# One in-projection pass for blocks 4 to 7, and a work timetable levelled for TensorE, in a hybrid attention and expert-retrieval kernel

## The reference

```python
h = rmsnorm(x)                                   # per token
q, k, v, xc, B, C = split(h @ w_in, 6)           # w_in: 1024 x 3072
sb = stick_breaking(rmsnorm(q), rmsnorm(k), v)   # 8 heads of 64, strictly causal
cv = B * causal_depthwise_conv3(C * xc)          # 512 channels
x = x + concat(rmsnorm(sb), rmsnorm(cv)) @ w_out
h2 = rmsnorm(x)
s1, s2 = (h2 @ w_q) against two tables of 128 sub-keys, for 8 heads
idx, gate = top 16 of the sums of the top 16 + 16, softmax over them
x = x + sum over 8 x 16 picks: gate * gelu(peer_u[idx] . h2) * peer_v[idx]
```

## Time and profile before

| | |
|---|---|
| median of 3 runs | 2874.86 us |
| the profiled execution: its time, and its span | 2879.8 us, 2878.0 us |
| busy: PE, DVE, ACT, POOL | 77%, 69%, 38%, 38% of the span |
| bytes moved by DMA | 1183.89 MB, mean 411 GB/s |
| of these by the gathers (q0), by SP's queue (q1) | 1073.81 MB, 108.17 MB |
| first dot | 104 us after the span's start |
| granted clock of TensorE, mean | 0.893 |

### The profile page before, as it was taken

How to read it: one execution, slowest core, us unless ns; L and a number is a source line. 1 busy time by engine, 2 the same in 40 slices (tenths; PEclk the granted TensorE clock), 3 DMA queues, 4 the chain that set the end, 5 groups by cost and what they waited for, 6 DMA issues and landing times. The chain is left out here.

```text
span 2878.0 us, 29917 instructions
## 1 busy us (share of the span) xinstructions
PE 2225.2 (77%) x9210; PEld 1012.2 (35%) x9210; DVE 1983.9 (69%) x4782; ACT 1093.7 (38%) x3164; POOL 1103.9 (38%) x1037
## 2 busy tenths in 40 slices
PE   9788889778977887778986888777898656555555
PEld 6535525333532343333542244333354111111111
DVE  3757766787666668786767666888666666666654
ACT  2333432552333335562333334666233322322222
POOL 0333433343343334443344333444334444434442
PEclk9999999989998998899998999999999776777787
DMA  9999999999999999999999999999999999999998
GB/s 390 359 413 403 398 419 418 419 412 412 385 421 420 419 419 412 419 415 416 412 420 420 418 410 416 410 417 415 419 405 420 416 422 419 421 418 416 415 421 353
DMA packets 178865, 1183.89 MB, mean 411 GB/s; under 512 B 19856, under 2 KB 21520, under 8 KB 47632
## 3 DMA queue, kind: packets, MB, share of 16 engines
q0 software_dynamic: 147456, 1073.81, 90.5%
q1 hardware_dynamic: 31248, 108.17, 9.6%
HBM read 1177.70 MB, written 4.19 MB: 411 GB/s over the span
## 5 line engine op out<-in xcount | busy, mean ns | idle before, releaser
L1472 DVE CUSTOM_DVE_ANT_0 ring<-ring,h2r 128x1024 f32<-128x1024 f32 x1024 | 1249.0, 1223 | 781.2 <-DMA ring<-table_uv,idx_t 772.1
L643 POOL DMA_INDIRECT ring<-table_uv,idx_t x1024 | 1102.0, 1076 | 1755.0 <-DVE dots L1472 1128.9
L911 PE MATMUL acc<-ring,wmask 128*64 128x512 f32 x4096 | 1200.6, 715 | 578.2 <-ACT wmask L1069 574.2
L911 PEld LDWEIGHTS acc<-ring,wmask 128*64 128x64 f32 x4096 | 283.4, 153 | 1286.4 <-ACT wmask L1069 845.9
L1064 ACT ACTIVATE dots<-dots 128x2 f32<-128x2 f32 x512 | 104.1, 203 | 1530.5 <-DVE dots L1472 1528.0
L1069 ACT ACTIVATE wmask<-gmask,dots 128x64 f32<-128x64 f32 x1024 | 300.3, 340 | 48.6 <-ACT dots L1064 1.5
L1057 ACT ACTIVATE gmask<-stack,gate_t 128x64 f32<-128x64 f32 x1024 | 293.1, 334 | 0.6 <-DVE gate_t L1459 0.5
L666 PE MATMUL pt<-hT,w_held 128*128 128x256 f32 (+1 forms) x560 | 109.3, 344 | 0.0
L666 PEld LDWEIGHTS pt<-hT,w_held 128*128 128x128 f32 x560 | 88.2, 193 | 28.2 <-issue 21.1
L1064 ACT ACT_TABLE_LOAD x73 | 93.7, 1283 | 1.3
L657 PE MATMUL pz<-w_ring,hT 128*128 128x512 f32 x192 | 90.8, 615 | 0.0
(11 more groups left out here) (274 smaller groups left out, 2171.6 us busy)
## 6 DMA issues: line engine op xcount, KB each, us to landing
w_ring<-wstream SPq DMA_DIRECT2D x121, 512.0 KB
ring<-wstream SPq DMA_DIRECT2D x32, 512.0 KB, 11.7
ring<-table_uv,idx_t POOLq DMA_INDIRECT x1024
w_held<-wstream SPq DMA_DIRECT2D x11, 512.0 KB, 13.4
xs<-x_in_dram SPq DMA_DIRECT2D x8, 512.0 KB
h2r<-wstream SPq DMA_DIRECT2D x8, 512.0 KB, 14.8
scores<-wstream SPq DMA_DIRECT2D x8, 512.0 KB, 15.4
xs<-wstream SPq DMA_DIRECT2D x4, 512.0 KB, 12.3
```

What stands on the lines that cost most here:

```text
L643: nc.gpsimd.indirect_dma_start(out=ring[:, cell(t):cell(t) + 2, :].rearrange("p c d -> p (c d)"), out_offset=None, in_=table, in_offset=ba ...
L911: mm = nc.tensor.matmul(acc[HALF * i:HALF * i + HALF, half * 512:(half + 1) * 512], wmask[:, slot, :], ring[:, cell(2 * p + i) + 1, half * ...
L1472: V.tensor_tensor_reduce(u, u, h2r[:, b % H_SLOTS, i, :], 1.0, 0.0, ALU.mult, ALU.add, dots[:, t % SLOTS:t % SLOTS + 1]).then_inc(dots_don ...
```

## The change

The in-projection (pieces 0 to 23) of supers 3 and 4 is made in one pass, in super 3 (`WIDE`), over its four blocks; super 4 (`LAST`) begins with its attention. In the pass each piece is used in four parts instead of two. The convolution works on 512 tokens at a time, and its steps stand before those of v (`ORDER`).

Room for the two additional blocks: their turned h lies in the parts of `kT` and `vals_sb` that belong to blocks 6 and 7 (`ahead_turned`), so the two pieces that were parked there for super 3 (33 and 36) are streamed. `cvT` and `qT` grow to four blocks, and `w_held` shrinks from 11 to 9 pieces (`LENT = 2`): pieces 37 and 38 lie in the new halves of `cvT` and `qT` up to super 2, and are streamed in supers 3 and 4. x of blocks 6 and 7 is loaded there for the pass (the step `ahead`), and a second time where it was loaded before, for the residual.

The stream has 103 pieces: 24 fewer for super 4, two more each for supers 3 and 4, and two more for super 3. With the two additional loads of x there are 16 transfers of 512 KB fewer.

`WHEN` gives super 2 less time (up to 212 and 254 instead of 224 and 262), super 3 begins at tick 254 instead of 262, super 4 at 524 instead of 521. `levelled()` is new: it takes the spread steps and moves a step to a later tick when TensorE's work, at 2.68 us a tick of which 0.97 us are the mix, would run more than 2.85 us behind.

```diff
-WHEN = [(-1, -1, 16), (8, 66, 84), (72, 224, 262), (262, 470, 514), (521, 732, 775)]
+WHEN = [(-1, -1, 16), (8, 66, 84), (72, 212, 254), (254, 473, 514), (524, 726, 775)]
+PART = 4.6
-H2_AT = {3: 266, 5: 518, 7: 790}
+H2_AT = {3: 260, 5: 518, 7: 790}
+ORDER = [list(range(PIECES)) for _ in SUPER]
+ORDER[WIDE] = [*range(PIECE_V), *range(PIECE_CONV, PIECE_OUT), *range(PIECE_V, PIECE_CONV), *range(PIECE_OUT, PIECES)]
+ORDER[LAST] = list(range(PIECE_OUT, PIECES))
+def parts_of(f, j):
+    return 4 if f == WIDE and j < PIECE_OUT else SUPER[f]
 def home(f, j):
-    if j >= FIRST_HELD:
+    if j >= FIRST_HELD + LENT or j >= FIRST_HELD and f < WIDE:
         return "held", j - FIRST_HELD
...
-        if f <= room + 1:
+        if f <= min(room + 1, WIDE - 1):
...
 def front_steps(f):
+    main = [(0.0, ("ahead",))] if f == WIDE else []
+    main += [(1.0, ("norm", blocks[0]))] if f != LAST else []
+    for b in blocks[1:] if f != LAST else ():
+        main += [pause(X_LATE if b >= X_SLOTS + 2 else 0), (1.0, ("norm", b))]
+    if f == WIDE:
+        main += [(1.0, ("norm", b)) for b in AHEAD]
+        main += [pause(1), (6.0, ("root1", blocks[0])), pause(4)]
+        for pair in (blocks, AHEAD):
+            main += [(2.0, ("h_scale", b)) for b in pair]
+        for pair in (blocks, AHEAD):
+            main += [pause(1)] + [(3.0, ("h", b)) for b in pair] + [(3.0, ("hT", b)) for b in pair]
+        main += [pause(1)] + w(*range(PIECE_K)) + [pause(1)] + w(*range(PIECE_K, PIECE_V)) + [pause(1)]
...
+        for c in range(1, CH):
+            j = PIECE_CONV + 3 * c
+            main += w(j, j + 1, j + 2) + [(4.0, ("conv", c))]
+        main += w(*range(PIECE_V, PIECE_CONV)) + [pause(1)] + [(3.0, ("qk_turn", b)) for b in AHEAD]
...
+TENSOR_TIME = {"w": 1.85, "v": 1.85, "scores": 1.8, "values": 1.4, "turn": 1.6, "h": 1.0, "qk_turn": 0.9, "x_turn": 1.1,
+               "key_scores": 1.4, "part": 0.3}
+TENSOR_TICK, TENSOR_SUM, TENSOR_LATE = 2.68, 0.97, 1.0
+def levelled(wanted):
+    out, queues, late = {}, [[] for _ in SUPER], 0.0
+    for tick in sorted(wanted):
+        for step in wanted[tick]:
+            queues[step[0]].append((tick, step))
+    for tick in range(min(wanted), BLOCKS * PICKS):
+        late = max(0.0, late + TENSOR_SUM - TENSOR_TICK) if tick >= 0 else 0.0
+        for queue in queues:
+            while queue and queue[0][0] <= tick:
+                step = queue[0][1]
+                needs = TENSOR_TIME.get(step[1], 0.0) if tick >= 0 else 0.0
+                if needs and late + needs > TENSOR_LATE + TENSOR_TIME["w"]:
+                    break
+                if step[1] == "h" and step[0] and queues[step[0] - 1]:
+                    break
+                late += needs
+                out.setdefault(tick, []).append(step)
+                queue.pop(0)
+    return out
...
 # ScalarE
-                if name == "norm":
+                if name == "norm" and i > 1:
+                    act.wait_ge(ahead_in, 32)
+                    act.wait_ge(piece_done, done(f - 1, PIECES - 1))
+                    nc.scalar.activation(spare[i - 2], lent[i - 2], ACT.Square, accum_out=ss1[:, i:i + 1]).then_inc(x_squared, 1)
+                elif name == "norm":
...
 # VectorE
                 if name == "root1":
-                    dve.wait_ge(x_squared, b0 + n)
-                    inverse_root(inv1[:, 0:n], ss1[:, 0:n], n, 1.0 / D, done=norm1)
+                    dve.wait_ge(x_squared, made_to(f))
+                    inverse_root(inv1[:, 0:made(f)], ss1[:, 0:made(f)], made(f), 1.0 / D, done=norm1)
 # SyncE
+                if name == "ahead":
+                    sp.wait_ge(piece_done, done(f - 1, FIRST_HELD + LENT - 1))
+                    for i, b in enumerate(AHEAD):
+                        sp.dma_start(lent[i], x[b * P:(b + 1) * P, :]).then_inc(ahead_in, 16)
```

277 lines of the change are left out of this document (177 added, 100 removed).

## The result

Five runs each: 2889.59 us (2889.3 to 2894.44) against 2874.86 (2872.92 to 2875.57), a ratio of 1.0051 [1.004, 1.0063]. The forecast was 2856, the range 2842 to 2869. The profiled execution took 2894.4 us (span 2892.6), 14.6 above that of before.

The account below looks back on a forecast made before the run. Gathers at 421 GB/s were taken as the bound. Terms -19.9 - 3.5 - 4.0 + 2 + 7 + 4 - 5 = -19.4 us from the profiled 2879.8, less 4.9, gave 2856 us; range 2842 to 2869.

Parts of the forecast that it names:

- Bytes: Whole kernel: 16 transfers fewer, 8.39 MB at 421 GB/s, shorten the time by 19.9 us.
- End of super 1: From tick 48: levelling spreads TensorE's pieces over 42 ticks, gain 3.5 us; bounds 6.5 gain to 3 loss.
- signs of being wrong: Below 400 GB/s in super 3's attention, no dip at tick 258, or super 1's end as slow as before.
- Attention of super 2: Eight passes in 31 ticks instead of 48, DVE's same passes in less room: adds 2 us, bounds 0 and 6.
- End of super 2: Key scores six ticks earlier, so DVE's wait for them goes: gain 4.0 us, bounds 5.2 and 0.
- Start of super 3: Tick 258: ACT waits for block 5's x before its norm, and the DMA queues run dry: 7 us lost, bounds 0 and 12.
- Super 3: In-projection stays DMA-bound, attention loses 0.3 us a pass, 8 with the handover against 4.2 before: loss 4 us.
- Super 4: 48 parts fewer and attention in 143 ticks instead of 98: gain 5 us, bounds 8 and 0.
- super 3 gives it back: Rival: super 3's attention pass costs 0.8 us more than the gathers, 13 us, its start 12: 2869 us; chance 0.11.
- an attention in series: Rival: super 3's passes can't overlap, 13.7 us each, 99 us in the place of 5: 2950 us; chance 0.03.
- first view: DMA row with GB/s below: DMA share stands at 9 in every slice while GB/s runs from 359 to 422.

Follow-up runs that it names:

- run 13: The changed kernel with the last 16 streamed pieces of weights loaded twice each, one load after the other: 2913.3 us, ratio 1.0143.
- run 2: The changed kernel without the levelling of TensorE's steps, all else as changed: 2876.20 us, ratio 1.0003.
- run 15: The kernel of run 14 without the rooms of two or three ticks written in by hand: 2869.16 us, ratio 0.9984.
- run 14: The changed kernel with block 5's norm four ticks later, levelling budget 2.85 us, super 3's parts closer, and rooms of two or three ticks: 2865.71 us.
- run 1: The changed kernel with the norm of block 5 five ticks later, tick 263 in the place of 258: 2879.39 us, ratio 1.0011.
- run 3: The changed kernel with block 4's first stick at least five ticks behind its scores, and the convolution's sums four pieces earlier: 2884.37 us, ratio 1.0025.
- run 5: The changed kernel with a levelling that never puts a step without TensorE work nearer to the step ahead than the timetable wanted: 2898.74 us, ratio 1.0074.
- run 10: The changed kernel with levelling budget 2.85 us and super 3's handover four ticks later, its distances kept: 2885.22 us, ratio 1.0049.
- run 11: The changed kernel with levelling budget 2.85 us, both second-pair q and k transposes in tick 382, scores, stick and sums one tick later: 2879.94 us, ratio 1.0027.
- run 12: The changed kernel with super 3's second scores three ticks behind the first, tick 389 for 387, first stick and sums following: 2880.71 us, ratio 1.0025.
- run 9: The changed kernel with only the first scores of super 3 four ticks later, tick 390 in the place of 386: 2877.96 us, ratio 1.0016.

## Why the prediction was wrong

*Bytes, -19.9.* Right: 20.0 by the bytes of the table, 16 to 26 by run 13, which adds a little lateness to the bytes. A stage that loses nothing moves 421 GB/s here too (the window from 720.8). The Trainium skill, "DMA: Bandwidth & Descriptors", section Bandwidth, gives about 358 GB/s, by which the bytes would be an estimated 23.4 us; but the same section gives that figure for two cores that stream at once, and measured 425 on one core alone. This kernel runs on one core, so the trace disagrees with the reading in the prediction and not with the section.

*End of super 1, -3.5.* Wrong: +1.8 in the first profile, +0.3 by the mean of seven, and 391 GB/s as before, which was one of the prediction's own signs of being wrong. I had priced it as load over time, 0.17 us a tick too much for TensorE (by its own terms 93.7 us in 35 ticks, 2.68 a tick and not 2.66). Levelling spreads the load over more ticks and doesn't change the loss: 6.7 us without it (run 2), 6.9 with it. So the load of a tick doesn't set it; what does stays open.

*Attention of super 2, +2 (bounds 0 to 6).* Mis-sized: 7 to 9. Run 2 gives back 3 of it, the room of two ticks before the last sum of squares 4 (ticks 176 to 192 lose 5.6 us in run 15 and 1.5 in run 14, which adds the rooms). There `sb_turn` and `sb_sum` stand in one tick, TensorE waits 3.5 us for ACT's square and mixes at 3.68 us behind it. I had priced DVE's busy time and no wait.

*End of super 2, -4.* Right in mechanism, -5.8: the scores wait is gone, and nothing took its place. In run 2 the key scores stand early too, without the levelling, and 3.4 us are lost there: by these losses the earlier scores are worth 2.7 and the levelling 3.1.

*Start of super 3, +7 (0 to 12).* Right in mechanism, mis-sized: 11.8, and run 1 removes it. I let the queues refill with the dot of tick 259, after 5.2 us without bytes. They were empty or nearly so for some 7 us, and thin for 12 us more, in which POOL waits once again (3.3 us lost, which I had at under 2). The landing time was 8.4 us (issue 851.47, ACT 859.89), as in the earlier trace rows. The Trainium skill, same page, section "Anatomy of one DMA", has 2.0 us and the bytes at 436 GB/s for a transfer that GpSimd issues; x is loaded by SP. Taken as an estimate here it would be 3.2 us, and this term nothing; the trace has 8.4 beside full queues, and that decides.

*Super 3, +4 (-2 to +15).* The step that failed: the overlap at the handover from in-projection to attention, of which the sum had at most 3 us. Of my 8 us, 16 passes of 0.3 made 5 and the handover with the in-projection 3. It was the other way round: ticks 400 to 432, at three ticks a pass, lose 0.3 us in all, so the pace that I feared is free in this kernel; handover and in-projection lose 23.3, the handover alone 17.2, and all of super 3 is +21.5, outside the bound. The in-projection's part is the first convolution step (4.9 us), where DVE's wider steps, which the prediction put at nothing, hold up ACT and by it the mix. I had compared each engine's busy time with the gathers' pace, and not read the order of tick 385 to 387: ACT, transpose, ACT, transpose, scores, mix, then ACT again, scores, sums, and the next mix only behind them. Runs 3 and 5 excluded the stick's distance as the only cause, run 10 the place, run 11 the shared tick, and run 12 the backlog as the only cause; what is left, was forecast for run 12 (3 to 7 us; 7.3 measured, with a time nearly 3 us over the 2878 expected) and shows in POOL's rows is two mixless stretches in a row. Why the loss is 10 in one kernel and 17 in another isn't settled by their lengths alone (run 3 has 14.6 and 14.8 us and loses 10.1, run 5 has less and loses 12.3), and the clock's part isn't separated.

*Super 4, -5.* -5.1 from tick 544 on, all of it ahead of tick 800, but +3.2 at its first scores, where the second scores (tick 526) wait 5.5 us for ACT's sigmoids of the first. Two rooms of three ticks behind the first scores remove it: 2.8 to 3.6 us in every profile without them, -0.1 to 1.8 with them.

The rivals: no rival had the handover. The two on the slower side (super 3 gives it back, an attention in series) priced the pace of a pass, the wrong mechanism; the handover stood only in the forecast's own term, which had 3 us for it and the in-projection together, against 23.3. One reading of the first view was off as well: the last slice stands at 8 and 353 GB/s, so the range is 353 to 422; nothing rests on it.

## What to carry to other kernels

Where one engine serves a ring and a chain that goes to another engine and back, price each junction by the time between two services of the ring, read from the order, and not by busy time per stage. Here one stretch of 14 to 17 us without a service cost 3 to 7 us and two in a row 10 to 17, so a planner that spreads load should also forbid two round trips between neighbouring services. Its budget should not be below the length that ticks have where it acts: 2.68 us against 2.84 pushed steps together and cost 13 us at the handover, which 2.85 gave back. More isn't better everywhere: 3.1 us lost more at super 1's end. And look behind the place that a move repairs: of the kernels in the table of run 12 all but two lose 2 to 13 us more in ticks 400 to 464 than the changed kernel.

## What the runs showed of the hardware that was not expected

TensorE's granted clock falls right behind a stage in which TensorE was busy 250 of 273 us (0.97 over that window). In the handover it waits 4.6 us for ACT, and then eight transposes take 1.94 us (1.06 at the full level, in run 5 at 1211.8), scores 2.50 (1.34), 16 matmuls of one column 3.41 (1.84 in run 12), x added into `acc` 3.62 (1.88), a pair's mix 3.27 to 3.68 (1.94). So the half level lengthens the handover by TensorE's own work. An estimate from the rows of all its work between 1215.9 and 1243.2, each less its time at the full level, is 10 us of the 27. In run 9, with the first scores in tick 390, the scores ran at the full level and the window at 0.84 instead of 0.76. Which of the two, the clock or the order, has the larger part in the 17 us wasn't separated.
